# One matrix product of a decoder step as seven half-size products, run ahead of the products it gates, and a final normalisation in three token groups

## The reference, cut to what matters

```
z = RMSNorm(x) @ w_in                      # 1024 -> 8192: the inputs of four branches, and four gates of 1024 columns
A, B, C, D = four branches of width 512 (pooling, short convolution, spatial gating, long convolution + LayerNorm + swish)
gates  = sigmoid(z[:, 4096:] + b_gate)     # T x 4 x 1024
merged = sum over k of gates[k] * (branch[k] @ w_branch[k])
x += merged @ w_mix_out
x += cross attention(RMSNorm(x))
x += relu(RMSNorm(x) @ w_ff1)^2 @ w_ff2    # 1024 -> 4096 -> 1024
y  = RMSNorm(x) * norm_f_g
```

## Time and profile before

| | us |
|---|---|
| median of three runs | 2258.83 (2258.67 to 2261.02) |
| profiled execution, its own time | 2257.59 |
| its span, first to last instruction | 2255.9 |
| PE busy | 2181.3 (97%) |
| DVE busy | 1237.0 (55%) |
| POOL busy | 823.7 (37%) |
| ACT busy | 595.9 (26%) |
| granted TensorE clock, mean | 0.993 of full speed |

### The profile page before, as it was taken

How to read it: one execution, slowest core, us unless ns; L and a number is a source line. 1 busy time by engine, 2 the same in 40 slices (tenths; PEclk the granted TensorE clock), 3 DMA queues, 4 the chain that set the end, 5 groups by cost and what they waited for, 6 DMA issues and landing times.

```text
span 2255.9 us, 34688 instructions
## 1 busy us (share of the span) xinstructions
PE 2181.3 (97%) x14272; PEld 2119.9 (94%) x14272; DVE 1237.0 (55%) x1417; ACT 595.9 (26%) x947; POOL 823.7 (37%) x599
## 2 busy tenths in 40 slices
PE   6999999999999999999999999998999999999997
PEld 5998899999999999999999986798999999899997
DVE  5558899653121222213455263269988886864763
ACT  5331222122101010111111172014333334333334
POOL 6114100004444434444444302145544444544541
PEclk9999999999999999999999999999999999999999
DMA  7522332122212112111311214321443448744322
GB/s 211 150 75 84 130 113 99 58 87 98 67 57 66 58 57 67 47 47 46 117 47 47 92 30 168 113 91 58 161 154 131 144 147 271 246 152 157 120 70 80
DMA packets 220344, 237.59 MB, mean 105 GB/s; under 512 B 8120, under 2 KB 181176, under 8 KB 218151
## 3 DMA queue, kind: packets, MB, share of 16 engines
q1 hardware_dynamic: 201814, 203.17, 27.9%
q10 hardware_dynamic: 18145, 32.57, 4.2%
q0 software_dynamic: 256, 0.01, 0.0%
HBM read 177.53 MB, written 58.67 MB: 105 GB/s over the span
## 4 chain that ended last, share of the span: by engine, by line
PE 88%; DVE 6%; DMA 2%; ACT 1%; issue 1%; POOL 0%; ACTq 0%; SPq 0%; DVEq 0%; POOLq 0%
PE PS L1057 53%; PE PS L1496 13%; PE PS L1543 13%; PE PS L1444 1%; PE PS L1406 1%; DVE opnd L2668 1%; DVE slots_d L2232 1%; PE PS L1377 1%; PE PS L1126 1%; PE PS L1088 1%; DMA xring<-in_x_prompt 1%; PE PS L1419 1%; PE PS L1362 1%; DVE w_lo L2255 1%; DMA hid_scratch<-stage 0%
## 5 line engine op out<-in xcount | busy, mean ns | idle before, releaser
L894 POOL TENSOR_TENSOR w_hi<-w_raw,ones 128x512 fp32r<-128x512 f32 x150 | 175.7, 1171 | 802.8 <-PE PS L1057 757.6
L1543 PE MATMUL PS<-opnd,slot 128*128 128x272 f32 x2688 | 342.5, 289 | 4.9 <-DVE opnd L2668 3.6
L1496 PE MATMUL PS<-opnd,slot 128*128 128x272 f32 x2688 | 341.2, 289 | 5.5 <-DVE opnd L2668 2.0
L1496 PEld LDWEIGHTS PS<-opnd,slot 128*128 128x128 f32 x2688 | 339.5, 189 | 6.9 <-issue 4.5
L1543 PEld LDWEIGHTS PS<-opnd,slot 128*128 128x128 f32 x2688 | 340.3, 189 | 5.7 <-DVE opnd L2668 4.1
L1057 PE MATMUL PS<-h_hi,w_hi 128*128 128x364 f32 x1512 | 337.1, 331 | 6.1 <-DVE w_lo L2255 5.8
L1057 PE MATMUL PS<-h_hi,w_lo 128*128 128x364 f32 x1512 | 334.0, 329 | 0.0
L1057 PE MATMUL PS<-h_lo,w_hi 128*128 128x364 f32 x1512 | 333.9, 329 | 0.0
L959 POOL TENSOR_TENSOR slot<-raw_A,slot 128x512 fp32r<-128x512 f32 x160 | 239.5, 1503 | 242.0 <-ACT slot L1556 241.6
L2503 DVE TENSOR_TENSOR tmp<-PS,tmp 128x728 f32<-128x728 f32 x64 | 43.4, 720 | 431.3 <-PE PS L1057 431.3
L1057 PEld LDWEIGHTS PS<-h_hi,w_hi 128*128 128x128 f32 x1512 | 260.5, 188 | 12.0 <-issue 10.1
(11 more groups left out here) (323 smaller groups left out, 3107.8 us busy)
## 6 DMA issues: line engine op xcount, KB each, us to landing
w_raw<-in_w_in SPq DMA_DIRECT2D x64, 512.0 KB, 4.0
hid_scratch<-stage SPq DMA_DIRECT2D x16, 1904.0 KB, 6.6
opnd<-hid_scratch SPq DMA_DIRECT2D x56, 544.0 KB, 6.4
raw_A<-in_w_ff SPq DMA_DIRECT2D x64, 256.0 KB, 3.1
raw_A<-in_w_ff SPq DMA_DIRECT2D x32, 512.0 KB, 4.6
branch_scratch<-oring ACTq DMA_DIRECT2D x16, 544.0 KB, 2.8
xring<-in_x_prompt SPq DMA_DIRECT2D x16, 512.0 KB, 6.0
w_raw<-in_w_branch SPq DMA_DIRECT2D x16, 512.0 KB, 3.5
```

The lines of the kernel that those rows point to most:

```text
L894: nc.gpsimd.tensor_tensor(w_hi[:, z % 2, cols], w_raw[:, z % 2, cols], ones[:, 0:1].broadcast_to([P, 512]), ALU.mult).then_inc(w_hi_done, 1)
L1496: mm = mmul(product_of(u, p)[:, c, :], w, x[:, HC * c:HC * c + HC], start=(j == 0 and e == 0), stop=(j == PAIRS - 1 and e == 2))
L1543: mm = mmul(product2_of(t)[:, c, :], w, x[:, part, HC * c:HC * c + HC], start=(j == 0 and e == 0), stop=(j == 2 * PAIRS - 1 and e == 2))
```

## The change

Gates are taken out of the loop over branches. They become sixteen units (UG = 16) of 256 gate channels, each in seven half-size products, all of them before the first branch product. The token operands of four of the seven (5, 6, 7, 4) are sums and differences of quarters of h, made while stage B still runs: 5 and 6 by POOL, their rounding by ACT; 7 by DVE and 4 by POOL as soon as the D branch has been read out of the region they take. Weight sums are formed by DVE, rounded by ACT, and POOL subtracts. Seven results per unit are combined by DVE, ACT puts the sigmoid on, and SP stores the two rows of gates of a unit to device memory. In the branch loop each of the 32 gate rows is read back into one of two buffers (`gate_load`), and whole branches are loaded by SP in place of single rows (`branch_load`). ACT's reading of D (Silu) is moved ahead of the store of the last B row. At the end, the last product runs its two token halves one after the other, and tokens 512 to 1087 are normalised in two groups, tiles 4 and 5 and tiles 6 to 8.

```diff
-Y_GROUPS = [[0, 1, 2, 3], [4, 5, 6, 7, 8]]
+Y_GROUPS = [[0, 1, 2, 3], [4, 5], [6, 7, 8]]
+UG = 16
+ORDER_IN = (1, 6, 2, 3, 5, 7, 4)
+ORDER_G = (1, 6, 7, 5, 4, 2, 3)
```

SP's list:

```diff
+        def gate_store(u):
+            sp.wait_ge(g_squashed, 4 * u + 4)
+            for r in range(2):
+                sp.dma_start(hid_dram[u][:, T * r:T * r + T], gate_rows(u, r)).then_inc(g_out[u % 2], 16)
+        def branch_load(q):
+            if q < 2:
+                for p in ((5, 6), (7, 4))[q]:
+                    sp.wait_ge(g_done, gate_done(UG - 1, p))
...
+            for ct in range(CT):
+                if q:
+                    sp.wait_ge(br_in[ct], 16 * 5 + 16 * q)
+                sp.dma_start(br_lo_f[q % 2][:, ct, :], br_dram[BRANCHES[q], ct]).then_inc(br_in[ct], 16)
+        def gate_load(x):
...
+                sp.wait_ge(gated, x - 1)
+            sp.wait_ge(*gate_stored(c // 2))
+            sp.dma_start(tmp[1 + x % 2][:, :], hid_dram[c // 2][:, T * (c % 2):T * (c % 2) + T]).then_inc(g_in[x % 2], 16)
+        for u in range(UG):
+            for block in ("A11", "A12", "A21", "A22"):
+                gate_weights(block, u)
+            if u >= 1:
+                gate_store(u - 1)
+        branch_slab(0)
+        branch_load(0)
+        branch_slab(1)
+        branch_load(1)
+        gate_store(UG - 1)
+        gate_load(0)
+        gate_load(1)
+        for x in range(2, 16):
+            branch_slab(x)
+            gate_load(2 * x - 2)
+            gate_load(2 * x - 1)
+            if x in (6, 10):
+                branch_load(x // 4 + 1)
```

POOL's list:

```diff
+        for j in range(PAIRS):
+            gate_t12(j)
+        for j in range(PAIRS):
+            gate_t12_lo(j)
+        gate_t4(0)
+        gate_t4(1)
+        for p in (1, 6, 2):
+            gate_lo(0, p)
+        gate_t4(2)
...
+        for u in range(1, UG):
+            for p in ORDER_G:
+                gate_lo(u, p)
```

PE's list:

```diff
-        for q in range(4):
-            bh, bl = br_hi[q % 2], br_lo[q % 2]
-            with pe.Fori(0, 2) as i:
...
+        for u in range(UG):
+            for p in gate_order(u):
+                pe.wait_ge(g_w_lo, gate_done(u, p))
+                gate_bank_free(u, p)
+                for j in range(PAIRS):
+                    if u == 0:
+                        gate_operand_ready(p, j)
...
+                            mm = mmul(gate_product(u, p)[:, c, :], w, x[:, HC * c:HC * c + HC],
+                                      start=(j == 0 and e == 0), stop=(j == PAIRS - 1 and e == 2))
+                mm.then_inc(g_done, 1)
+        for x in range(32):
...
+            product(n, S_GATE + x // 2, br_hi[q % 2], br_lo[q % 2], kts=CT, ofs=lambda kt, x=x: (2 * kt + x % 2) * P,
+                    wait_slab=(x % 2 == 0), arrive=(br_lo_done, 4 * q) if x % 8 == 0 else None)
```

DVE's list, first in the fourth round of B ahead of the drain of its last product, then the units and the branch loop:

```diff
+            if ct == 3:
+                for p in (7, 6, 3):
+                    gate_sum(0, p)
+                gate_t3(0)
+                gate_t3(1)
...
+        for u in range(1, UG):
...
+            gate_p6(u)
+            if not last:
+                for p in (7, 6, 3):
+                    gate_sum(u + 1, p)
+            gate_p7(u)
...
+            v.tensor_tensor(c22, gate_product(u, 5), two(u3), ALU.add)
+            v.tensor_tensor(c12, gate_product(u, 5), two(u2), ALU.add).then_inc(g_taken, 1)
+            if not last:
+                gate_sum(u + 1, 5)
+            gate_p4(u)
+            gate_p2(u)
+            if last:
+                branch_lo(0, 0)
...
+        for x in range(32):
...
+            dve.wait_ge(g_in[x % 2], 32 + 16 * (x // 2 + 1))
+            if x == 0:
+                for u in (UG - 2, UG - 1):
+                    dve.wait_ge(*gate_stored(u))
...
+            if q < 3 and m >= 4:
+                branch_lo(q + 1, m - 4)
```

DVE's end:

```diff
-        quarters_added(T2 - 1)
-        y_root(1)
-        for t in Y_GROUPS[1]:
-            y_scaled(t)
...
+        v.tensor_tensor(c12[:, 0, :], c12[:, 0, :], product2_of(t)[:, 0, :], ALU.add).then_inc(c12_first, 1)
+        dve.wait_ge(wino, half_done(2 * t + 1))
+        v.tensor_tensor(c12[:, 1, :], c12[:, 1, :], product2_of(t)[:, 1, :], ALU.add).then_inc(taken, 1)
+        for G in (1, 2):
+            y_root(G)
+            for t in Y_GROUPS[G]:
+                y_scaled(t)
```

More of the change, by code:

```diff
@@ L70 @@
 S_GATE = S_B + 12
-S_MIX = S_GATE + 48
+S_MIX = S_GATE + 16
 S_Q = S_MIX + 8
@@ new lines, in _ @@
+        n = N_A_MAP[CT - 1]
+        pool.wait_ge(ready[n % 2], n // 2 + 1)
+        pool.wait_ge(kv_stored, 8 * 16)
+        pool.wait_ge(state_out, 16 * (2 + 9 + 1 + 9))
+        for j in range(PAIRS):
[7 more added lines that the diff above has]
+        gate_t4(2)
+        gate_lo(0, 3)
+        gate_t4(3)
+        gate_lo(0, 5)
+        gate_lo(0, 7)
+        gate_lo(0, 4)
@@ L1302, in _, with gate_bank_free @@
         tails("tail_b", SCONV_H, 3 * CT)
-        for q in range(4):
-            bh, bl = br_hi[q % 2], br_lo[q % 2]
-            with pe.Fori(0, 2) as i:
[L1307 to L1315, removed]
+        def gate_bank_free(u, p):
+            b, before = GATE_BANKS[u, p]
+            if before is None:
+                if b == 3:
+                    pe.wait_ge(aux_drained, AUX["tail_b"] + 1)
+                if b in (1, 2):
+                    pe.wait_ge(*accumulated(N_B_C[3], drained))
+                if b in (0, 1):
+                    pe.wait_ge(*accumulated(N_B_B[3], drained))
+            elif before[1] == 1:
+                pe.wait_ge(g_p1, before[0] + 1)
+            else:
+                pe.wait_ge(g_taken, gate_drained(*before))
@@ L1548, in _ @@
                         rows[2 * q + h]()
+        t = T2 - 1
+        bank_free(t)
+        pe.wait_ge(w_op_lo, half_done(2 * t + 1))
+        for c in range(2):
+            for j in range(2 * PAIRS):
+                w_slot, x = slot[RING2[(2 * t + j // PAIRS) % 5]], held(I2 - 1, j)
+                wh, wl = w_slot[:, 0, j % PAIRS, :], w_slot[:, 1, j % PAIRS, :]
+                for e, (w, part) in enumerate(((wh, 0), (wh, 1), (wl, 0))):
+                    mm = mmul(product2_of(t)[:, c, :], w, x[:, part, HC * c:HC * c + HC],
+                              start=(j == 0 and e == 0), stop=(j == 2 * PAIRS - 1 and e == 2))
+                if c == 1 and j == PAIRS - 1:
+                    final_rows("yD", Y_GROUPS[1], Y_BANK, 0)
+            mm.then_inc(wino, 1)
+            if c == 0:
+                rows[6]()
+        final_rows("yE", Y_GROUPS[2], Y_BANK + 1, 1)
     @block.scalar
@@ L1876, in residual_tiles @@
+        branch_hi(0, 2)
+        branch_hi(0, 3)
+        for q in range(1, 4):
+            for ct in range(CT):
+                branch_hi(q, ct)
+        for m in range(KT):
+            act.wait_ge(gated, 24 + m + 1)
+            copy(mv_hi[:, m, :], merged[:, m, :]).then_inc(mv_hi_done, 1)
         def residual_tiles(n0):
@@ L2144, in _ @@
             if i == I2 - 1:
-                for h in range(2):
+                for h in range(2 if q < 3 else 1):
                     rows_out[2 * q + h]()
@@ new lines, in _ @@
+        gate_sum(0, 5)
+        gate_t3(2)
+        gate_t3(3)
+        gate_operand_lo(7, 0)
+        gate_operand_lo(7, 1)
+        gate_p6(0)
+        gate_operand_lo(7, 2)
+        gate_operand_lo(7, 3)
+        gate_p2(0)
+        c12, c22 = two(gate_quarter(0, "12")), two(gate_quarter(0, "22"))
+        gate_operand_lo(4, 0)
+        gate_operand_lo(4, 1)
+        gate_stage_free(0)
+        dve.wait_ge(g_done, gate_done(0, 3))
+        v.tensor_tensor(c12, gate_product(0, 3), two(u2), ALU.add).then_inc(g_taken, 1)
```

549 lines of the change are left out of this document (411 added, 138 removed).

## The result

The changed kernel takes 2238.97 us (median of 4 runs, 2237.17 to 2240.45), the kernel before beside it 2259.32 us (4 runs, 2258.67 to 2261.02): ratio 0.9908, 95% interval 0.9891 to 0.9926. The gain is 20 us; 40 were forecast, and the range ended at 2238.0. The profiled execution of the changed kernel took 2237.17 us, its span is 2235.4 us.

The account below looks back on a forecast made before the run. PE was taken to bound the kernel, busy without a gap through the gates. Terms -46.5 + 5 + 3 + 1 - 2 = -39.5 us gave 2218.1 us profiled, 2219.3 us median; range 2210 to 2238 us.

Parts of the forecast that it names:

- Gate products: Gate matmuls on PE: 2304 removed (384.0 us), 2688 narrower ones added (337.5 us); gain 46.5 us.
- second rival: Gate units: preparation by other engines paces each unit, 22.5 us instead of 21.1; 2241.7 us, chance 0.07.
- Rival four: Gate matmuls: each costs the same at either width, 64 us more; 2323 us, chance 0.01.
- Removed around B: Stage B: removed row work and POOL's 28 operand operations in its idle time cost PE 0.
- Entry: From B to the gates: DVE drains B's last product late, product 6 waits; 5 us lost, bounds 0 to 11.
- Gates to branches: First branch product after the gates: queued loads and rows through ACT and DVE come late; 3 us lost.
- rival three: Branch stage: gate rows come back too late through two buffers, slower than before; 2272 us at 11.5 us landing, chance 0.03.
- Inside the branch stage: Entries to branches three and four: PE may wait at the fourth depth block; 1 us lost (0 to 3).
- The end: After PE's last matmul: a tail of 13.3 us instead of 15.2; gain 2 us (0 to 3.5).
- Rival one: Both seams dear: 11 us lost at the gates' entry, 15 in the load queue before branches; 2237.3 us, chance 0.14.

Follow-up runs that it names:

- run 1: Changed kernel with POOL's operand operations working on 16 columns instead of 544 (output not the reference's); 2219.80 us, ratio 0.9828.
- run 6: Changed kernel with `gate_t12` and `gate_t12_lo` moved from POOL to DVE in stage B, `gate_t4` left on POOL; 2229.33 us, ratio 0.9869.
- run 2: Changed kernel with POOL's `gate_t12` and `gate_t12_lo` made to wait until after the mean and variance sums; 2239.40 us, ratio 0.9917.
- run 4: Changed kernel with DVE making the next branch row's low half before adding the gated product to the sum; 2234.75 us, ratio 0.9893.
- run 8: Kernel before with only the new end (three normalisation groups, last product's halves in turn); 2256.85 us, ratio 0.9991.
- run 9: Changed kernel with all operand operations on DVE, branch low halves ahead of the sum, and DVE's and ACT's entry queues reordered; 2216.44 us, ratio 0.9812.
- run 3: Changed kernel with the drain of B's last product ahead of `gate_t3` and ACT copying product 1 before product 7's operands; 2241.83 us, ratio 0.9927.

## Why the prediction was right or wrong

- **Gate products, -46.5 us: right.** 0.1255 us a matmul, PE without a gap over units 1 to 15, 21.1 us each. The step that the second rival doubted (DVE, ACT and POOL keep up) held with room: DVE was busy 115.80, POOL 133.21 of 302.00 us. Rival four fell with it.
- **"Removed around B ... 0": this step failed.** It counted POOL's 28 operations as work in POOL's idle time and left "a few us of room on DVE if POOL slows it". The idle engine was the right one to look at; the price was not POOL's time but DVE's. B lost 6.8 us, at two waits and at the lower clock behind the first. Runs 1 and 6 show the cause by two ways, run 2 that it moves with the work. The prediction had the sign of it in its own rows: L2790 at 1729 ns beside busy POOL, where the same kind of operation with an operand from `PS`, L2733, takes 720; and the mean of L2510 there, 1777 ns, hides two durations (shown in the next section). It used the first for the gate units and the entry, and not for B. The Trainium skill, "GPSIMD Engine Reference", section "1. Specifications", says that GpSimd shares its memory interfaces with VectorE, with contention for VectorE's instructions in a two-port mode or with two inputs from the on-chip memory. The rows of run 1 agree (1285 to 2422 ns with two such inputs, 901 against 903 with one from `PS`); the multiplication by a scalar, 744 to 1850 ns, has one such input and would have to be of the first kind, which no run here shows.
- **Entry, 5 us: mis-sized, 13.0 us** (350.5 - 337.5), above its upper bound of 11. The place, the waiter and the cause of lateness were as written: product 6 waits for its bank, the drain is late behind sums and `gate_t3`. But the value was taken nearer the undisturbed end of 0 to 11, and the disturbed one applied, since `gate_t4` runs on POOL at the same time: 340.0 us in run 1, so 10.5 of the 13.0 us come from POOL's operand work, and from `gate_t4`, since run 6, which leaves only that on POOL, keeps the 350.5 us. And behind the gap PE ran 24 matmuls at the lower clock, 2.5 us that no term held.
- **Gates to branches, 3 us: right in size**, 2.7 us, **in part by luck**. The sum had 1.7 us for the first gate row and 1 to 2 us for the branch rows passing ACT and DVE. The gate row came late, but PE did not wait for its drain; the branch rows alone took the 2.7 us. A gate row lands after 4.0 us (median of the 32), so rival three fell as well.
- **Inside the branch stage, 1 us: 3.3 us** by run 4, 2.8 of them waits, just above its bounds of 0 to 3. The place was right; the sum that stands ahead of the low half on DVE was not in the term, and run 4 takes just that away.
- **The end, -2 us: right**, -2.0 us in run 8's trace and -2.4 in its median. The tail is 12.1 us where the term had 13.3, but PE ends 1.1 us later, which it did not hold; the two nearly cancel.
- **Rival one** gave 2237.3 us, near the result, in part by other terms: its 15 us in the load queue did not come, its 11 us at the entry were 13, and B, which it did not name, had the rest.

With the measured terms: -46.5 + 6.8 + 13.0 + 2.7 + 3.3 - 2.4 = -23.1 us; the spans differ by 20.5, and B's later start in that profile, 2.8 us, is nearly the difference. Without POOL's operand work the forecast of 2219.3 us would have been met: run 1 took 2219.8 us, with 2.5 us lost at the entry where the sum had 5, and more than the sum had in the branch stage.

## What to carry to other kernels

Work put on an idle POOL is not free if DVE works beside it on operands in the on-chip memory: count what it adds to DVE's operations, and compare it with DVE doing the work in its own gaps. Look in the old trace for one and the same DVE operation at two durations; the difference is the price. In the kernel before, the sum of L2510 is one: 12 of its 24 run beside a POOL operation and take 2262 ns on average, the 12 others 1292 (its line's view, with the shortest, the median and the longest):

```profile
L2510 DVE TENSOR_TENSOR merged<-merged,tmp x24: 1291/1776/2271, 697.0 to 1098.9; 128x1088 f32 x24
```

Where several engines prepare an entry in turn, reorder all their queues together, since moving one link here only moved the wait.

## What was not expected of the hardware

- A DVE operation of 64 columns costs 1352 ns beside POOL instead of 243, one of 1024 columns 1850 instead of 744: 1.1 us more in either case, so short operations suffer most for their size.
- POOL's work saves DVE nothing here: 20 operations on POOL made DVE busy 42.30 us in 48 us, and with 18 operations more on DVE itself (15 of those 20 among them) it was busy 40.38 us.
- A gap of 8.6 us on PE cost 2.5 us more behind it (24 matmuls in 5.53 us, clock 0.89 in that stretch); in run 9, whose gaps are below 1 us, the clock of the stretch is 1.00. Behind the gaps of 2.3 to 2.8 us in B the lower clock came in some profiles and not in others: from 433 to 472 us the clock is 0.96 in the changed kernel and 1.00 in run 3, from 472 to 522 us it is 1.00 and 0.97.
